# A 64-byte spacer in front of the first buffer of low Strassen weights

## The reference

```python
mod = (silu(c) @ w_ada + b_ada).reshape(3, 3, 1024)          # shift, scale, gate of three parts
h = modulate(rms_norm(x, norm_ffn1_g), mod[0, 0], mod[0, 1])
x = x + 0.5 * mod[0, 2] * swiglu(h, ffn1_w_in, ffn1_w_out)   # first FFN, 2 x 2816 columns in, 2816 rows out
h = modulate(rms_norm(x, norm_mix_g), mod[1, 0], mod[1, 1])
proj = h @ w_mix_in                                          # 1536 columns
x = x + mod[1, 2] * (concat(pool_mixer(proj), gmlp(proj)) @ w_mix_out)
h = modulate(rms_norm(x, norm_ffn2_g), mod[2, 0], mod[2, 1])
x = x + 0.5 * mod[2, 2] * swiglu(h, ffn2_w_in, ffn2_w_out)   # second FFN
return rms_norm(x, norm_final_g)
```

## Time and profile before

| | |
|---|---|
| median of 3 runs | 876.66 us (875.43 to 879.33) |
| profiled execution, first to last instruction (span) | 874.8 us |
| TensorE busy | 845.0 us, 97% |
| VectorE busy | 641.4 us, 73% |
| ScalarE busy | 379.8 us, 43% |
| GpSimd busy | 50.4 us, 6% |
| mean granted TensorE clock | 0.991 |

### The profile page before, as it was taken

One profiled execution on the slowest core, in us unless ns is written; L12 is line 12 of the kernel. 1 busy time (PEld: TensorE's weight loads), 2 busy tenths in 40 slices (PEclk: granted clock), 3 DMA queues, 4 the chain that ended last, 5 costly groups with the idle time before them and its releaser, 6 DMA issues.

```text
span 874.8 us, 14160 instructions
## 1 busy us (share of the span) xinstructions
PE 845.0 (97%) x5767; PEld 755.0 (86%) x5767; DVE 641.4 (73%) x919; ACT 379.8 (43%) x528; POOL 50.4 (6%) x56
## 2 busy tenths in 40 slices
PE   4899989999999999999999999999999999999996
PEld 3678869888999998888887898899988899999886
DVE  4579977776788877858747779988794588885443
ACT  6233325312466653134424256656511356665323
POOL 0000000000001000000350000000000000100000
PEclk9999998999999999999999999999999999999999
DMA  9997565586566665943534422576663566663222
GB/s 276 291 309 235 160 177 155 167 264 173 133 157 157 160 183 178 299 130 97 154 99 125 143 74 73 140 181 173 193 208 98 137 171 159 155 158 104 86 67 96
DMA packets 214797, 142.02 MB, mean 162 GB/s; under 512 B 6232, under 2 KB 193740, under 8 KB 214732
## 3 DMA queue, kind: packets, MB, share of 16 engines
q1 hardware_dynamic: 209780, 132.19, 52.1%
q0 software_dynamic: 4896, 8.92, 6.2%
q10 hardware_dynamic: 56, 0.01, 0.0%
HBM read 130.08 MB, written 2.10 MB: 151 GB/s over the span
## 4 chain that ended last, share of the span: by engine, by line
PE 81%; DVE 9%; DMA 3%; SPq 2%; issue 2%; ACT 1%; DVEq 0%; ACTq 0%
PE ps L1669 13%; PE ps L1671 13%; PE ps L1670 13%; PE ps L1846 12%; PE ps L1842 12%; PE ps L1844 12%; DVE work L1130 2%; DMA ada_first<-in_w_ada_dram 1%; PE ps L1968 1%; PE ps L1969 1%; PE ps L1970 1%; SPq L469 1%; DVE h_lo L1077 1%; DVE xs L1070 1%; DMA sw_raw<-in_ffn_w_in_dram 1%
## 5 line engine op out<-in xcount | busy, mean ns | idle before, releaser
L1842 PE MATMUL ps<-sums_hi,sw_hi 128*128 128x256 f32 x544 | 152.4, 280 | 4.2 <-ACT ev L832 4.2
L1844 PE MATMUL ps<-sums_lo,sw_hi 128*128 128x256 f32 x544 | 152.9, 281 | 0.0
L1669 PE MATMUL ps<-b_hi,sw_hi 128*128 128x512 f32 (+1 forms) x374 | 143.4, 383 | 0.0
L1670 PE MATMUL ps<-b_lo,sw_hi 128*128 128x512 f32 (+1 forms) x374 | 141.5, 378 | 0.0
L800 ACT CAST sw_hi<-sw_raw 128x1024 fp32r<-128x1024 f32 (+2 forms) x102 | 119.8, 1180 | 31.6 <-DVE sw_raw L1251 19.2
L1842 PE MATMUL ps<-h_hi,sw_hi 128*128 128x256 f32 x408 | 114.3, 280 | 3.0 <-DVE sw_lo_a L1264 3.0
L1846 PE MATMUL ps<-sums_hi,sw_lo_a 128*128 128x256 f32 x408 | 115.7, 284 | 0.0
L1844 PE MATMUL ps<-h_lo,sw_hi 128*128 128x256 f32 x408 | 114.6, 281 | 0.0
L1842 PEld LDWEIGHTS ps<-sums_hi,sw_hi 128*128 128x128 f32 x544 | 102.9, 189 | 4.6 <-issue 4.1
L1264 DVE TENSOR_TENSOR sw_lo_a<-sw_raw,sw_hi 128x1024 fp32r<-128x1024 f32 x68 | 98.9, 1455 | 9.9 <-ACT sw_hi L800 7.6
L1844 PEld LDWEIGHTS ps<-sums_lo,sw_hi 128*128 128x128 f32 x544 | 102.7, 189 | 0.0
(11 more groups left out here) (193 smaller groups left out, 1571.8 us busy)
## 6 DMA issues: line engine op xcount, KB each, us to landing
sw_raw<-in_ffn_w_in_dram SPq DMA_DIRECT2D x170, 256.0 KB, 4.2
sw_raw<-in_w_ada_dram SPq DMA_DIRECT2D x15, 1024.0 KB, 5.6
sw_raw<-in_ffn_w_out_dram SPq DMA_DIRECT2D x32, 384.0 KB, 4.5
sw_raw<-in_ffn_w_out_dram SPq DMA_DIRECT2D x32, 320.0 KB, 3.4
w_raw<-in_ffn_w_in_dram SPq DMA_DIRECT2D x19, 512.0 KB, 5.4
ada_raw<-in_w_ada_dram SPq DMA_DIRECT2D x18, 512.0 KB, 5.4
sw_raw<-sw_raw POOLq DMA_DIRECT2D x34, 256.0 KB, 3.3
ada_first<-in_w_ada_dram SPq DMA_DIRECT2D x14, 512.0 KB, 7.3
```

What stands on the lines that cost most here:

```text
L1669: nc.tensor.matmul(dst, w_h, a_h, start=start, stop=False)
L1670: nc.tensor.matmul(dst, w_h, a_l, start=False, stop=False)
L1842: nc.tensor.matmul(dst, w_h[:, k, :], src_hi[:, k, :], start=start and k == 0, stop=False, skip_group_check=True)
L1844: nc.tensor.matmul(dst, w_h[:, k, :], src_lo[:, k, :], start=False, stop=False, skip_group_check=True)
```

## The change

A tensor of 16 float32 values in each partition, 64 bytes, is named in front of sw_lo_a. Nothing writes or reads it.

```diff
         sums_lo = sb("sums_lo", [P, 4, KA, TH], F32R)
         b_hi = sb("b_hi", [P, GF, T], F32R)
         b_lo = sb("b_lo", [P, GF, T], F32R)
+        aside = sb("aside", [P, 16])
         sw_lo_a = sb("sw_lo_a", [P, 5 * BL], F32R)
```

## The result

The changed kernel takes 871.52 us (median of 6 runs, 865.89 to 872.35) against 876.75 us (median of 6, 875.43 to 879.33) for the kernel before. The ratio is 0.992, interval 0.990 to 0.995: 5.2 us faster, where 878.8 us and a range from 871.5 us were forecast. The time lies on the lowest edge of that range, and on the other side of the kernel before than the forecast's sum: the forecast of "no difference" was wrong. In the profiled execution the span fell from 874.8 to 866.3 us.

What follows compares the result with a forecast made beforehand. TensorE, busy 97% of the span, was taken as the bound; slow pace in 20 Strassen tiles adds 2.1 us, other terms 0, to the 876.66 us median: 878.8 us, range 871.5 to 881.0.

Steps and rivals of the forecast that it cites:

- no difference: Whole kernel: the time lies between 872.3 and 881.0 us, not measurably different from before; chance 0.78.
- What bounds the kernel: TensorE, busy 97% of the span: only closer matmul starts or a removed wait could pay.
- A pace, once taken, holds until something stops the stream: TensorE's matmul streams: slow 117.8 ns stays for at least 50 aligned matmuls; 512-column streams hold theirs longer.
- Take the displacement away, and the shift is gone too: Tiles 3 to 13 and 23 to 33 enter slow and stay slow: +0.107 us in 20 tiles, +2.1 us.
- The row leaned on for the entry: The last mixer product, 256-column matmuls after 512-column ones: 50 distances at 117.8 ns, none fast.
- The second rival: Strassen low weights: address plays no part, or the displaced pattern stays modulo 256; 876.7 us, chance 0.12.
- the first rival: Strassen tiles: all run at the fast pace, 9.52 us a tile; 9.7 us less, 867.0 us, chance 0.13.
- each may come out either way: Tiles behind stalls: +0.2 or -0.5 us for tiles 1 and 2, 0 or -2.6 for 16 to 22; taken as 0.
- The third rival: Second products turn from 228.9 to 233.3 ns: 4.4 us, with slow tiles 6.7 us more, 883.4 us; chance 0.06.
- the buffer makes no difference at 512 columns: Second products: 228.9 ns whether weights come from sw_lo_a or sw_lo_b, so no gain was taken there.
- VectorE's 6 ns: VectorE's writes take 1224 ns into sw_lo_a, 1218 into sw_lo_b; some 80 writes, 0.5 us in all, counted as nothing.
- lines of 16 bytes: SBUF: a start at 64 modulo 128 lies on a line as well as one at 0, so worth 0.

Runs made afterwards that it cites:

- the kernel steered with 128 columns: The changed kernel with an added, overwritten matmul of 128 columns in front of tiles 1 and 16 alone; 868.46 us, ratio 0.992 against the kernel before.

## Why the prediction was wrong

**What bounds the kernel** was read rightly: the gain is distance between TensorE's matmuls, in the tiles named.

**"A pace, once taken, holds until something stops the stream"** was right. In the Strassen tiles of the change, of its repeats and of the kernels with added matmuls, a pace held over whole stretches, and what ended one was a wait, another kind of product, the first displaced load behind such a product, or an added matmul.

**The step that failed** is "Take the displacement away, and the shift is gone too. Tiles 3 to 13 and 23 to 33 would then enter slow and keep it." The change took no displacement away. It moved sw_lo_a from 64 bytes away from the other weights, modulo 256, to 128. The kernels with 192 and 448 bytes, which do take it away, behave as forecast: the same entry, 117.8 ns, 9.89 us a tile. With 128 bytes between them the first load from sw_lo_a in tiles 3 and 23 took the stream to 113.3 ns instead, and the tiles take 9.52 us. The word "aligned", for all that is 0 modulo 128, joined two cases that the address table's last column kept apart. The row leaned on for the entry, the mixer's last product on w_split, has high and low weights at one residue: it was the nearest row for 192 bytes, not for the change. The second rival named this very column, but let the old pattern stay; what the new distance does, no row of before could show.

**The size of the first rival.** It gave 9.7 us less, and the tiles' share came out at 9.2 in the profiled execution. The median gained 5.2 us, and 6.9 when it was measured again. Part of the difference is the prediction's own remark on tiles behind stalls, that "each may come out either way": tiles 16 to 22 took 9.52 us in one profiled execution and 9.96 in the other, 7 x 0.44 = 3.1 us, so that the tiles' share was 9.2 us in the one and 6.1 in the other, and added matmuls move the choice. It is not the whole spread between executions: the end of tile 0 moves by more than a microsecond, and the half clock in tile 15, 3.41 us long in both, begins 0.4 us behind the wait in the first execution and 1.3 us behind it in the second.

**The second products** kept 228.9 ns in their first group (198 matmuls from 168.81 to 214.13 us in the changed kernel), as taken. The third rival came in small: the first product behind tile 33 took 233.5 ns (793.29 to 800.76 us, 32 distances), as did the first behind tiles 13 and 22, where the kernel before has 230.0 to 230.1. Over all second products it is 229.6 ns for 229.3, 0.3 us. That "the buffer makes no difference at 512 columns" held for the kernel before, and failed with the spacer of 128 bytes (in its first group 230.9 ns on sw_lo_a, 229.1 on sw_lo_b). VectorE's 6 ns were nothing, as taken. What was taken from the Trainium skill, "SBUF — State Buffer" (Door 1: The DMA port swizzle), by whose lines of 16 bytes the change would be worth 0, holds for VectorE's writes (into sw_lo_a 1224 ns displaced and 1225 aligned) and not for TensorE, where the measurement decides: spacers of 64, 128 and 192 bytes gave the long stretches three patterns, none of them that of before.

**What stays open**: why. That the weights' read and the moving operand's read meet somewhere in a pattern of 256 bytes would fit the rows, but no view shows these reads. Nor is it known what phase a stream has when it leaves a wait.

## What to carry to other kernels

Where TensorE is busy all the time, read the distance from start to start: the same instruction on the same address had 113.3 or 118.9 ns here (in other blocks 113.3 or 117.8), up to 5%, and the shown durations hardly tell. In this kernel the residues modulo 256 of stationary and moving operands decided which of these a stream could have, and its entry which it had; so an edit elsewhere that shifts an entry cost or won up to 10 us without touching the loop. A forecast from one kernel's rows should list every residue class that its change leaves unequal, and one profiled execution should not be taken for the median.

## What was not expected of the hardware

- An idle tensor's size moved the time from 869.3 us (320 bytes) to 877.5 (192); the same 64 bytes in front of the activations made 885.5.
- A single added matmul of 128 or 192 columns sets the pace of the tiles behind it, ten of them up to the next second product, 9.52 or 9.96 us each.
- 512-column products have such paces too: 226.7, 228.9 and 233.3 ns. The plain products of the first FFN took 233.3 before and 228.9 in the changed kernel's profiled executions, on equal addresses; with the spacer of 192 bytes they took 229.0 and in the kernel steered with 128 columns 233.3, so the spacer does not decide it.
